# A two-model float32 chain on one core: seven PSUM banks and first norms a unit later, half-input units input by input, VectorE's half of the output in two pieces, and a new order of the steps

## The reference

```python
def rmsnorm(x, g):
    xf = x.astype(jnp.float32)
    y = xf * lax.rsqrt(jnp.mean(xf * xf, axis=-1, keepdims=True) + RMS_EPS)
    return (y * g.astype(jnp.float32)).astype(x.dtype)
...
def _sq_relu_mlp(h, w_up, w_down):
    u = jax.nn.relu(h @ w_up)
    return (u * u) @ w_down
```

## Time and profile before

| what | value |
|---|---|
| median of three runs | 817.16 us (815.79, 817.16, 817.36) |
| profiled execution, own time | 818.34 us |
| its span, first to last instruction | 816.5 us |
| mean granted clock of TensorE | 0.998 |
| instructions | 14785 |
| DMA | 137.83 MB, mean 169 GB/s |

### The profile page before, as it was taken

How to read it: one execution, slowest core, us unless ns; L and a number is a source line. 1 busy time by engine, 2 the same in 40 slices (tenths; PEclk the granted TensorE clock), 3 DMA queues, 4 the chain that set the end, 5 groups by cost and what they waited for, 6 DMA issues and landing times.

```text
span 816.5 us, 14785 instructions
## 1 busy us (share of the span) xinstructions
PE 802.5 (98%) x5848; PEld 746.8 (91%) x5848; DVE 600.9 (74%) x1137; ACT 550.1 (67%) x1043; POOL 0.2 (0%) x4
## 2 busy tenths in 40 slices
PE   8999999999999999999999999999999999999997
PEld 7999899999999899988999999999899888888886
DVE  7999998989978987777467374876767757555744
ACT  7886775699967888767446464768767675544643
POOL 0000000000000000000000000000000000000000
PEclk9999999999999999999999999999999999999999
DMA  8532435558454534454656365534443647435831
GB/s 323 189 110 104 130 104 181 190 159 271 150 188 155 158 128 147 163 186 151 207 181 202 154 226 174 174 118 140 156 155 129 216 145 283 168 120 179 286 101 51
DMA packets 39956, 137.83 MB, mean 169 GB/s; under 512 B 4560, under 2 KB 5328, under 8 KB 39888
## 3 DMA queue, kind: packets, MB, share of 16 engines
q1 hardware_dynamic: 38880, 135.45, 49.1%
q10 hardware_dynamic: 1008, 1.45, 0.5%
HBM read 135.83 MB, written 1.05 MB: 168 GB/s over the span
## 4 chain that ended last, share of the span: by engine, by line
PE 74%; DVE 12%; ACT 7%; DMA 3%; issue 3%; SPq 0%; DVEq 0%; ACTq 0%
PE bank L801 14%; PE bank L794 11%; PE bank L796 11%; PE bank L795 11%; PE bank L802 7%; PE bank L805 5%; PE bank L807 5%; PE bank L806 5%; DVE weights_lo L1746 3%; ACT weights_hi L1241 2%; DMA weights_raw<-stream_dram 2%; PE bank L1163 2%; ACT operand L1241 1%; DVE operand L1746 1%; DVE temp L1746 1%
## 5 line engine op out<-in xcount | busy, mean ns | idle before, releaser
L1241 ACT ACTIVATE weights_hi<-weights_raw 128x1024 fp32r<-128x1024 f32 (+3 forms) x255 | 258.4, 1038 | 91.1 <-DMA weights_raw<-stream_dram 33.1
L794 PE MATMUL bank<-operand,weights_hi 128*128 128x256 f32 (+1 forms) x1092 | 314.1, 288 | 3.4 <-DVE operand L1752 2.3
L1746 DVE TENSOR_TENSOR weights_lo<-weights_raw,weights_hi 128x1024 fp32r<-128x1024 f32 (+3 forms) x255 | 298.4, 1199 | 23.5 <-ACT weights_hi L1241 23.0
L796 PE MATMUL bank<-operand,weights_lo 128*128 128x256 f32 (+1 forms) x1092 | 309.6, 284 | 0.0
L795 PE MATMUL bank<-operand,weights_hi 128*128 128x256 f32 (+1 forms) x1092 | 309.2, 283 | 0.0
L794 PEld LDWEIGHTS bank<-operand,weights_hi 128*128 128x128 f32 x1092 | 206.1, 189 | 10.3 <-issue 5.7
L796 PEld LDWEIGHTS bank<-operand,weights_lo 128*128 128x128 f32 x1092 | 206.3, 189 | 0.0
L795 PEld LDWEIGHTS bank<-operand,weights_hi 128*128 128x128 f32 x1092 | 205.8, 188 | 0.0
L801 PE MATMUL bank<-operand,weights_hi 128*128 128x512 f32 x512 | 180.1, 394 | 0.0
L802 PE MATMUL bank<-operand,weights_lo 128*128 128x256 f32 x512 | 143.7, 281 | 0.0
L801 PEld LDWEIGHTS bank<-operand,weights_hi 128*128 128x128 f32 x512 | 96.2, 188 | 21.3
(11 more groups left out here) (212 smaller groups left out, 789.0 us busy)
## 6 DMA issues: line engine op xcount, KB each, us to landing
weights_raw<-stream_dram SPq DMA_DIRECT2D x244, 512.0 KB, 4.5
weights_raw<-stream_dram SPq DMA_DIRECT2D x6, 384.0 KB, 4.2
temp<-memT_dram SPq DMA_DIRECT2D x8, 256.0 KB, 3.9
residual<-xT_dram SPq DMA_DIRECT2D x3, 272.0 KB, 6.3
weights_raw<-stream_dram ACTq DMA_DIRECT2D x3, 256.0 KB, 5.7
constants<-consts_dram SPq DMA_DIRECT2D x1, 536.5 KB, 8.3
arena<-consts_dram SPq DMA_DIRECT2D x1, 512.0 KB, 7.0
out_dram<-arena SPq DMA_DIRECT2D x2, 256.0 KB, 2.5
```

The source lines that it names most:

```text
L794: e.matmul(to, w_h, x_h, start=start, stop=False, skip_group_check=True)
L796: return e.matmul(to, w_l, x_h, start=False, stop=stop, skip_group_check=True)
L1241: return e.activation(to, of, ACT.Copy, bias=0.0, **scale)
L1746: return e.tensor_tensor(to, a, b, op)
```

## The change

It does six things:

1. The first input projection uses seven banks in turn in place of six, and the first four units of the heads take other banks.
2. The norm "a" (of the first layer's input) has its mean behind unit 4 and its spread behind unit 5, each one later; the norms "q" and "kv" likewise, behind units 8 and 9. Units 1 to 5 are held in place of 1 to 4.
3. All half-input units go input by input: each input for both output tiles, then the next.
4. The first units of the MLPs go input by input too.
5. VectorE's half of the output of each row block is made in two instructions of 256 columns, and SyncE sends it in two DMAs of 128 KB.
6. The table `TIMES` is new throughout, so that ScalarE's and VectorE's steps stand in another order in many places. Of it the diff shows the rows `root` and `rstd`. Among the moves, `lambda_exp` (an exponential, line 1296, which loads its own table between the roots "a" and "q") goes from time 10.25 to 26.14, and ScalarE's list has one table load less in all, 20 in place of 21.

```diff
         n = {"a_uq": 2, "a_k": 4, "a_v": 3, "a_in": 1}[kind]
         if i < 4:
-            banks[kind, m] = ((5, 0), (1, 2), (3, 4, 5, 0), (1, 2, 6, 7))[i]
+            banks[kind, m] = ((4, 5), (0, 1), (2, 3, 4, 5), (0, 1, 6, 7))[i]
         else:
             banks[kind, m] = tuple((at + j) % 3 for j in range(n))
...
-    ("scalar", "root"): (7.5, 11.75, 11.88, 32.25, 34.75, 73.33, 101.33, 167.17, 193.33),
-    ("vector", "rstd"): (7.5, 11.5, 11.62, 32.25, 33.67, 71.67, 98.83, 162.83, 192.33),
...
+    ("scalar", "root"): (9.25, 14.12, 14.25, 33.5, 37.25, 74.33, 99.75, 165.33, 192.6),
+    ("vector", "rstd"): (9.08, 14.07, 14.21, 32.2, 35.5, 71.67, 98.8, 165.12, 192.33),
...
     a = AT["a_in", 0, 0, 0]
-    statistics(a + 3, "a")
+    statistics(a + 4, "a")
     vector("rope_rows_a")
-    hold(a + 5.06, range(a + 1, a + 5))
-    statistics(a + 7, "q")
-    statistics(a + 7, "kv")
+    hold(a + 6.06, range(a + 1, a + 6))
+    statistics(a + 8, "q")
+    statistics(a + 8, "kv")
...
             if w.kind == "a_in" and w.m0 < 11:
-                return [w.m0 % 6]
+                return [w.m0 % 7]
...
                 (b,) = bank_of(v)
                 if w.k0 == 0:
                     take(b)
-                turns = [(j, k) for j in range(2) for k in range(4)]
-                if w.kind == "out2" and w.layer == 0 and w.k0:
-                    turns.sort(key=lambda jk: jk[1])
-                for j, k in turns:
+                for k, j in itertools.product(range(4), range(2)):
                     tile = OUT2_INPUTS[w.k0 + k] if w.kind == "out2" and w.layer == 0 else w.k0 + k
...
-                for j, b in enumerate(bank_of(v)):
-                    if w.k0 == 0:
+                banks = bank_of(v)
+                for k, (j, b) in itertools.product(range(w.nk), enumerate(banks)):
+                    if k == 0 and w.k0 == 0:
                         take(b)
-                    for k in range(w.nk):
-                        wait_input(v, w.k0 + k)
-                        w_h, w_l = weights(v, k, j)
-                        i = two_sums(b, w_h, w_l, x[:, :, w.k0 + k, 0:SEQ], w.k0 + k == 0, w.k0 + k == 7)
-                    if w.k0 + w.nk == 8:
+                    wait_input(v, w.k0 + k)
+                    w_h, w_l = weights(v, k, j)
+                    i = two_sums(b, w_h, w_l, x[:, :, w.k0 + k, 0:SEQ], w.k0 + k == 0, w.k0 + k == 7)
+                    names = []
+                    if w.k0 + k == 7:
                         held_by[b] = [("evacuated", "up", w.layer, w.m0 + j)]
-                        names = [("sum", "up", w.layer, w.m0 + j)]
-                    else:
-                        names = []
-                    if j == w.nm - 1:
+                        names.append(("sum", "up", w.layer, w.m0 + j))
+                    if k == w.nk - 1 and j == w.nm - 1:
                         names.append(("unit", v))
                     if names:
                         i.then_inc(*done("sums", *names))
...
                 dve.wait_ge("rstd", "out", i)
-                stt(x_tok[:, i, 512:1024], x_tok[:, i, 512:1024], col, gain_row[:, 512:1024], ALU.mult, ALU.mult).then_inc(
-                    *done("outputs", ("out", i, 1)))
+                for half in range(2):
+                    at = slice(512 + 256 * half, 768 + 256 * half)
+                    stt(x_tok[:, i, at], x_tok[:, i, at], col, gain_row[:, at], ALU.mult, ALU.mult).then_inc(
+                        *done("outputs", ("out", i, 1 + half)))
...
             for i in range(2):
-                sp.wait_ge("out", i, 1)
-                load(out[i * P:(i + 1) * P, 512:1024], x_tok[:, i, 512:1024], "output_written", "written", i, 1)
-            sp.wait_ge("written", 1, 1)
+                for half in range(2):
+                    at = slice(512 + 256 * half, 768 + 256 * half)
+                    sp.wait_ge("out", i, 1 + half)
+                    load(out[i * P:(i + 1) * P, at], x_tok[:, i, at], "output_written", "written", i, 1 + half)
+            sp.wait_ge("written", 1, 2)
```

More of the change, by code:

```diff
@@ L1 @@
+import itertools
 from collections import defaultdict, namedtuple
@@ L228 @@
 TIMES = {
-    ("scalar", "root"): (7.5, 11.75, 11.88, 32.25, 34.75, 73.33, 101.33, 167.17, 193.33),
-    ("scalar", "row"): (8.5, 13.11, 13.22, 34.5, 36.5, 78.22, 73.67, 107.14, 167.33, 196.14),
-    ("scalar", "latent_hi"): (13.44, 13.78, 13.67, 13.56, 15.2),
-    ("scalar", "meta_latent"): (13.89, 15.8),
-    ("scalar", "small"): (11.25,),
-    ("scalar", "lambda_exp"): (10.25,),
-    ("scalar", "mla_softmax"): (20.29, 20.57, 23.6, 24.18, 24.55, 25.4, 28.29, 28.36),
-    ("scalar", "mla_turned"): (20.71, 23.8, 24.09, 24.64, 25.6, 28.21, 28.43, 28.5),
@@ L270 @@
-    ("scalar", "turned_residual"): (196.71, 198.33, 201.75, 203.6),
-    ("scalar", "square_out"): (250.5, 251.5),
-    ("vector", "total"): (0, 0, 0, 30.67, 0, 70.67, 98.67, 162.67, 189.9),
-    ("vector", "rstd"): (7.5, 11.5, 11.62, 32.25, 33.67, 71.67, 98.83, 162.83, 192.33),
-    ("vector", "rope_rows_a"): (10.5,),
-    ("vector", "latent_norm"): (11.81, 11.94, 11.75, 12.09, 12.27),
-    ("vector", "latent_rest"): (12.18, 12.73, 12.45, 12.55, 14.25),
-    ("vector", "small"): (4.5, 11.25, 11.38, 11.69, 41.4, 12.36),
@@ new lines @@
+    ("scalar", "small"): (7.5,),
+    ("scalar", "lambda_exp"): (26.14,),
+    ("scalar", "mla_softmax"): (21.17, 21.83, 23.25, 23.88, 26.21, 26.5, 26.86, 28.08),
+    ("scalar", "mla_turned"): (21.67, 23.5, 24.67, 26.36, 26.71, 27.5, 28.42, 28.5),
+    ("scalar", "mla_y"): (23.62, 26.57, 26.64, 26.93, 28.25, 28.58, 28.75, 28.83),
+    ("scalar", "memory"): (28.17, 28.92, 29.17, 29.67, 47.5, 48.08, 54.33, 54.67),
+    ("scalar", "taps"): (42.4, 40.75, 42.6, 42.8, 48.5, 48.25, 48.75, 48.92),
+    ("scalar", "inputs"): (48.33, 48.58, 59.5, 60.29),
@@ new lines @@
+    ("scalar", "inputs_root"): (48.83, 51.33, 60.43, 60.57),
+    ("scalar", "silu_gates"): (55.33, 60.86),
+    ("scalar", "y_b"): (59.75, 59.25, 60.71, 60.14, 62.33, 63.33, 63.67, 62.67),
+    ("scalar", "softmax"): (76.33, 76.67, 78.5, 78.17, 81.18, 81.09, 81.55, 81.64, 87.25, 87.12, 87.62, 87.75,
+        91.27, 91.09, 91.64, 91.36, 168.5, 168.75, 170.08, 170.42, 172.33, 172.17, 173.09, 173.36, 177.29, 177.36,
+        177.64, 177.57, 184.08, 184.17, 184.42, 184.58),
+    ("scalar", "softmax_scale"): (78.33, 78.83, 79.71, 79.14, 170.25, 170.17, 170.33, 170.67, 173.45, 172.67,
+        173.55, 173.82, 177.43, 177.5, 177.71, 177.86, 184.33, 184.5, 184.67, 184.92),
@@ new lines @@
+    ("scalar", "turned"): (79.43, 79.29, 81.27, 79.86, 81.45, 85.25, 90.25, 90.5, 91.91, 92.2, 170.5, 170.75,
+        170.83, 172.5, 173.73, 173.64, 177.07, 177.21, 177.79, 177.93, 178.17, 178.83, 184.83, 184.75, 186.2,
+        186.4),
+    ("scalar", "y_2"): (81.36, 81.82, 172.83, 173.27, 177.14, 178.33, 179.5, 180.67, 186.6, 186.8),
+    ("scalar", "diff_out"): (85.75, 86.5, 91.55, 91.82, 92.6, 93.17),
+    ("scalar", "sub_root"): (87.38, 92.4, 93.33),
+    ("scalar", "sub_scale"): (91.18, 92.8, 93.67),
@@ new lines @@
+    ("vector", "rstd"): (9.08, 14.07, 14.21, 32.2, 35.5, 71.67, 98.8, 165.12, 192.33),
+    ("vector", "rope_rows_a"): (9.83,),
+    ("vector", "latent_norm"): (14.57, 14.36, 14.43, 14.5, 14.71),
+    ("vector", "latent_rest"): (14.79, 14.64, 14.86, 16.12, 16.38),
+    ("vector", "small"): (4.5, 7.5, 9.17, 9.42, 34.67, 56.86),
+    ("vector", "mla_mask"): (19.5, 20.75, 21.33, 21.56, 22.2, 23.2, 25.13, 25.8),
+    ("vector", "mla_norm"): (20.25, 21.17, 21.44, 21.89, 23.4, 25.4, 25.47, 25.93),
+    ("vector", "mla_turned"): (21.11, 21.5, 21.94, 23.6, 25.33, 25.73, 26.12, 26.25),
```

91 lines of the change are left out of this document (38 added, 53 removed), and 52 rows, old and new, of the table TIMES.

## The result

The changed kernel takes 817.99 us in the median of 20 runs (816.99 to 819.16), the kernel before 816.34 us in 20 runs beside them (815.38 to 817.84). The ratio is 1.0019, 95% interval 1.0013 to 1.0025: slower by 1.6 us, where 1.6 us less was forecast. The profiled execution of the changed kernel took 817.39 us (span 815.6, clock 0.998). That of before, 818.34 us, lies above all 20 timed runs beside it.

A forecast was written before the change was run, and what follows sets the result against it. TensorE, busy 98% of the span, bounds the kernel, so only its waits can be gained. Terms −0.1 + 0 + 0 + 0 − 1.5 + 0 = −1.6 us: 816.7 profiled, 815.5 from the median, range 812.6 to 819.0.

The forecast's parts named there:

- The order searched anew: At 580 us, `arena` copied ahead of unit 178's weights: TensorE's 1.5 us wait goes; other moves 250 to 810 us, 0.
- First norms: Norm "a" a unit later: mean gains 0.3 us, spread loses 0.2, waiting 0.4 to 0.6; net −0.1, ends −0.5 and +0.5.
- The latents: Norms "q" and "kv" before unit 11, one unit of cover instead of two: 0, ends −0.5 and +2.3 us.
- Rival 3: Latents bind between spread "q" and unit 11: price 2.3 us, moba 2's 1.5 taken up, 819.4 us; chance 0.16.
- The heads: Up to 125 us: 0.16 wait at unit 28 goes, about 0.3 lost before `a_out`; net 0, ends −1 and +1.
- Input by input: Half-input units, unit 69 near 245 us: wait 1.26 falls to about 0.6, mean "in2_0" waits instead; 0, ends −0.7 and 0.
- Two pieces: Output at the end: first piece issued sooner, second later, ScalarE's 256 KB still ends last; 0, ends −0.2 and +0.4 us.
- Rival 4: Weight copies waiting for their DMA ahead of steps TensorE wants, three new places, 1.5 us each: 820.1 us; chance 0.06.
- Rival 2: Gain near 580 us taken up by what is late next, ScalarE or a DMA: 816.9 us; chance 0.22.

The follow-up runs named there:

- after_old_recurrent: Changed kernel with the table times from 32 to 65, the recurrent layer, as in the kernel before; ratio 0.9985 to the kernel before.
- after_old_gates: Changed kernel with the old times for ScalarE's and VectorE's steps whose old times lie from 45 to 58; ratio 0.9992 to the kernel before.
- before_memory: Kernel before with only ScalarE's two copies of the second memory's rows moved, the first ahead of unit 48's weight copy; ratio 1.0022 to the kernel before.
- before_again: Kernel before, unchanged, run again for a second profile; ratio 0.9987 to the kernel before.
- after_again: Changed kernel, unchanged, run again for a second profile; ratio 1.0013 to the kernel before.
- after_memory: Changed kernel with ScalarE's two copies of the second memory's rows back behind unit 48's weight copy; ratio 1.0017 to the kernel before.

## Why the prediction was wrong

**The order searched anew.** The mechanism at 580 us was right, to the copy of unit 178's weights that waits for its DMA. Its size was not: 1.0 us by the units, where 1.5 was taken from one execution, and this kernel's second profile had 1.21. The step that failed is another. The prediction weighed the moved steps "between 250 and 810 us" and the heads to 125, and put what moved from 125 to 245 at nothing without giving a reason; only the wait at 245 was weighed. The section on the change had even noted that ScalarE's list has one table load less in all, which hid that the recurrent layer has one more. This stage costs 1.8 us (0.76 and 1.05), and that turns a gain of about 0.5 us into a loss of 1.3. Shown by runs: its place ("after_old_recurrent"), that both losses come of moves between 45 and 58 ("after_old_gates"), and that a wait for the memory's rows can cost as much in the kernel before ("before_memory"), though taking that move back in the changed kernel gives nothing. Read from the traces but not tried by itself: the ninth table load as the cause at units 60 to 62. Open: how the loss at 49 to 51 divides over the 50 entries of the table that moved, and whether the load alone would cost 1.05. The moves behind 250 us were put at 0 beside the 1.5; they also lose 0.3 between units 70 and 170, inside the ends given.

**First norms.** Net −0.1 was forecast, with ends ±0.5. Up to unit 7 it is +0.17: mean "a" no longer waits, as forecast, but spread "a" waits 0.79, longer than the 0.4 to 0.6 of the walk. In executions that start late (−0.79 at unit 7 in the table) neither kernel waits at this norm, and the difference is nil.

```profile
27.69 0.56 PE L1090 MATMUL bank<-constants,cols 16*128 16x16 f32 x3 [0.79 <-DVE cols L1808]
```

**The latents** cost 0.39 at unit 14, inside the ends of −0.5 and +2.3. Rival 3's place was right, at a sixth of its price of 2.3: VectorE idles there for unit results and rows.

```profile
41.73 0.44 DVE L1744 TENSOR_TENSOR silu_gates<-bank,rows 128x272 f32<-128x272 f32 x1 [0.88 <-PE bank L798]
42.75 1.50 DVE L1744 TENSOR_TENSOR values<-values,rows 128x272 f32<-128x272 f32 x4 [0.57 <-ACT rows L1239]
```

**The heads** stand at 0 from unit 14 to 48, as taken, though the wait of the earlier trace rows grew to 0.78 and others went. **Input by input** was put at 0 because only unit 69 had a wait; it saves 0.4 to 0.6, since `b_out` and the last `out2` wait a little for each input. The wait at 245 that the step argued from was nearly absent elsewhere. **Two pieces** were put at 0, and come to 0.07 less: from the start of unit 251 to the end of the span the 15 profiles with two pieces read 29.43 to 29.45 us, the five with one 29.51 or 29.52. VectorE's pair takes 0.88. But the prediction's path was not right. It held that ScalarE's 256 KB still end last; they now land in 2.1 us (median of two) in place of 2.7, and SyncE's fourth transfer is issued 0.10 behind them, at 812.64, and lands last, at 814.68 against 814.31. Before, ScalarE's landed last, at 815.74 against 815.49. The smaller transfers land in 2.2 us in place of 2.5, and this makes up for the later issue.

```profile
811.73 0.88 DVE L1750 SCALAR_TENSOR_TENSOR arena<-arena,cols 128x256 f32<-128x256 f32 x2
811.79 0.72 ACT L1239 ACTIVATE arena<-arena,cols 128x512 f32<-128x512 f32 x1 [0.29 <-DVE cols L2131]
...
812.25 0.81 SPq L2388 DMA_DIRECT2D out_dram<-arena  x2
812.54 0.37 ACTq L1734 DMA_DIRECT2D out_dram<-arena  x1
```

```profile
out_dram<-arena SPq DMA_DIRECT2D x4, 128.0 KB, 2.2
out_dram<-arena ACTq DMA_DIRECT2D x2, 256.0 KB, 2.1
```

**The rivals.** Rival 4 came nearest in kind to what "before_memory" does, a copy that waits for its DMA ahead of steps that TensorE wants; but it looked at the weights' copies alone, and no run shows that such a wait makes the loss in the changed kernel. Rival 2 was right in part: of the 1.2 us that "before_again" waits at 580, 1.0 is won. None of the four looked at units 49 to 62, a stage in which no wait had been seen but the one at its end.

## What to carry to other kernels

A stage in which the bottleneck engine is 99% busy has next to nothing to gain from a new order and much to lose: walk the helpers' queues there first, and count table loads stage by stage, not over the kernel. Before a wait is priced from one profile, look at it in a second: the one at 580 us, which ends with a DMA, read 1.50, 1.21 and 0.53 us, and the one at 245 us 1.26 and nearly nothing. And when the waits list doesn't explain a difference, compare the starts of the work units: the loss shows to 0.1 us.

## What the runs showed of the hardware

- The wait for the first weights varies between executions: in "after_again" TensorE stood 1.93 us until 9.99 us, in "before_again" 0.70 until 8.62. After the longer one the granted clock read 0.66 from 10 to 15 us, part at 1.2 and part at 2.4 GHz, and 1.00 again from 15 us. Five of the 20 profiles are like this, with waits of 1.74 to 2.27 us, and unit 3 starts at 18.95 to 19.48 us in them, against 16.55 to 17.56 in the others. The length of the wait does not decide it alone: "after_memory" stood 1.83 us until 9.37, and its clock stayed at 1.00. In the five the wait at the first norm is gone, which gives 0.79 back against "before_again" (the −0.79 of the table). Their mean clocks are 0.996 and 0.997, as in the 32 timed executions that are 1.4 us longer; whether all of those have this start-up is not shown, since they were not traced.

```profile
10.00:15.00 5.00, 5.00 (x27) 5.00 (x28) 4.86 (x10) 4.32 (x11) 0.00 (x0) 0.66 1.03 403
```

- One function table load takes ScalarE 1.28 us in every place of every trace (409 loads), and the next instruction follows at once: in the changed kernel a copy ends at 196.96, the load runs from 196.98, and the silu starts at 198.28. By the traces, TensorE paid most of one additional load, some 20 us later; the load alone was not tried.
